# Prompt attention and sample attention of a decoder step in one written-out pipeline of 80 units

## The chip, the core and the metric

The kernel runs on one NeuronCore of a Trainium2 chip. The metric is device time in microseconds (us), median of three runs. The engines, each with a queue of its own: TensorE (PE, with its weight loads as PEld), VectorE (DVE), ScalarE (ACT), GpSimd (POOL) and SyncE (SP, which only starts transfers here). They meet at semaphores. Matmul results go to eight banks of PSUM, 512 fp32 values per partition each.

## The reference, cut to what matters

The model is a two-layer decoder step for a prompt of 1040 tokens (16 learned ones and 1024) and, with the same weights, eight samples of 8 new tokens over 512 cached ones. Layer 0 has a convolution branch and an attention branch of 8 heads of width 64:

```
s = einsum('bqhd,bkhd->bhqk', q, k) * 64**-0.5      # and a bias c_q - c_k per head, c = cumsum(log forget gate)
p = softmax(where(pos_k <= pos_q, s + bias, -inf))
att = einsum('bhqk,bkhd->bqhd', p, v)               # prompt: 1040 x 1040 causal; sample: 8 x 520, cache read through a page table
conv_out = silu(layer_norm(depthwise(a)))           # over 512 channels
mix = concat([conv_out, att]) @ w_out               # then residual, layer norm, SwiGLU, layer norm
```

Layer 1 has other mixers and is not touched. Outputs are fp32.

## The kernel before, in words

Activations lie transposed, channels on partitions, T = 1104 columns (1040 of the prompt, 64 of the samples), in three chunks of C = 368. Large products split each fp32 operand into a high and a low fp32r part and run three matmuls (`mm3`, L670 to L672). The program is in stages: input and projections; keys and values written out; prompt attention; sample attention; output product; SwiGLU; layer 1.

**Prompt attention.** A unit is one head and one tile of 128 queries (tile 8 has 16): `att_units`, 72 units, with the keys up to the diagonal, 128 to 1040 of them. Every engine runs the same step number n over all units, written out, and in order:
- PE: `scores` of unit n (L823, L825 for the mask, L827; fp32r) into banks 0-2 or 3-5 in turn; `turn` of unit n-2 (L840: transposes of the exponentials through banks 5 and 6); `values` of unit n-3 (L859: transposed probabilities as 128-column weights, 64 value columns moving, into bank 2 or 7 in turn); and at some steps `back` (L868), a transpose of a finished 128-column result of two heads.
- DVE: `inverse` (L1681) of the row sum of unit n-1, `peak` (L1677, the row maximum) of unit n, `turned` (L1687, a PSUM copy), parts of the next head's operands (`head_low`, L1497, L1707, L1710) and the copy behind `back` (L1695).
- ACT: `expo` (L1186) of unit n, `turned` (L1193) for bank 6, `result` (L1200), which scales the value product by the inverse row sum, and `head_high` (L1211).
- POOL does nothing in it (255.7 us without work).

**Sample attention** comes after it and takes one sequence at a time, in loops: 32 transposes of cached keys (`turn_keys`, L895) copied by ACT (L1241); `sample_scores` (L907 to L909); maximum (DVE L1742), exponential (ACT L1245), normalisation (DVE L1747); transposes (L918), copies (ACT L1250); `sample_values` (L925: the cache's values as 128-column weights, 16 columns moving). Between them stands the layer norm of the convolution branch, chunk by chunk (products L684 and L685 with a matrix of 1/512, DVE L1755, L1758, L1762, ACT L1274, L1277, and Silu L1281). Its buffers lie where those of prompt attention were, so SP starts the cache's loads when that has ended.

**Output product** (`out_product`): four pairs of input tiles in the order OUT_TILES[0] = (0, 1, 2, 3), where 0 and 1 are the convolution's and 2 and 3 the attention's. ACT rounds them to the high part (L1292), DVE makes the low part (L1497). The first weights are split long before.

Of the kernel before, what the change touches and what calls it, by code (L numbers as in the profile page):

```python
# [14 lines left out]
P = 128  # L15
# [48 lines left out]
OUT_TILES = ((0, 1, 2, 3), (0, 2, 1, 3))  # L64
# [7 lines left out]
PV0 = 64 * (NPAGE + 1)  # L72
ORDER = (tuple(range(9)), (0, 8, 1, 2, 3, 4, 5, 6, 7))
# [26 lines left out]
def build(nc, t):  # L100

    ctx = ExitStack()
    with ctx:
# [27 lines left out]
        SSM, _ = at("SSM", o, [P, HT, NS, NQ])  # L131
# [5 lines left out]
        SELC, _ = at("SELC", o, [P, NS, NH, NQ])  # L137
# [10 lines left out]
        YSM, o = at("YSM", o, [P, 2, C])  # L148
# [3 lines left out]
        ATT, o = at("ATT", B0 + 8 * T * 4, [P, 2, NTT, P])  # L152
        assert o <= R0
        YCA, o = at("YCA", B0 + 8 * T * 4, [P, HT, C])
        SQA, o = at("SQA", o, [P, HT, C])
        YSA, o = at("YSA", o, [P, 2, C])
        RSA, o = at("RSA", o, [P, C])
# [16 lines left out]
        QS1, o = at("QS1", A0, [P, 2, TP], F32R)  # L174
        KS1, o = at("KS1", o, [P, 2, TP], F32R)
        QS2, o = at("QS2", o, [96, 2, TP], F32R)
        PB, o = at("PB", o, [P, 3, TP])
        assert o >= stage_end
        VP, o = at("VP", o, [P, 2, NTT, P])
        PT, o = at("PT", o, [P, 2, NTT, P])  # L180
        KS2, o = at("KS2", o, [96, 2, TP], F32R)
        QBA, o = at("QBA", o, [32, TP])
        IDR, o = at("IDR", o, [P, P], F32R)
        MKR, o = at("MKR", o, [P, P], F32R)
        ST4, o = at("ST4", o, [P, 3, 72])
        LFO, o = at("LFO", o, [P, NTT, NH])
        assert o <= B0

        KR, o = at("KR", A0, [P, 2, NPAGE, HALF])
        VR, o = at("VR", o, [P, 2, NPAGE + 1, HALF])  # L190
        KTS, o = at("KTS", o, [P, 2, HT, KS])
        PSA, o = at("PSA", o, [64, 2, KS])
        PTS, o = at("PTS", o, [P, 2, NPAGE + 1, 64])
        QBD, o = at("QBD", o, [P, 2, 328])
        LFS, o = at("LFS", o, [64, KS])
        KBS, o = at("KBS", o, [P, KS])
        SLS, o = at("SLS", o, [P, 2, 64])
        CQ2, o = at("CQ2", o, [P, NQ])
        ST5, o = at("ST5", o, [64, 2, 8])
        assert o <= B0  # L200
# [46 lines left out]
        def row(k, r):  # L247
# [23 lines left out]
        qk_done, nm_ready, exp_done, rc_ready = sem("qk_done"), sem("nm_ready"), sem("exp_done"), sem("rc_ready")  # L271
        back_done, back_evac = sem("back_done"), sem("back_evac")
# [4 lines left out]
        kr_in, vr_in = [sem("kr_in0"), sem("kr_in1")], [sem("vr_in0"), sem("vr_in1")]  # L277
        sk_done, kt_ready, kt_new, qbd_zero, qbd_ready, sls_ready = (sem("sk_done"), sem("kt_ready"), sem("kt_new"),
                                                                     sem("qbd_zero"), sem("qbd_ready"), sem("sls_ready"))
        sqk_done, snm, sexp, s_inverse, spn = sem("sqk_done"), sem("snm"), sem("sexp"), sem("s_inverse"), sem("spn")  # L280
        spt_done, spt_ready, spv_done, satt = sem("spt_done"), sem("spt_ready"), sem("spv_done"), sem("satt")
        la_sum, la_mean, la_cen, la_sq, la_sum2, la_var, la_sd, la_rs, la_nrm, la_act, la_hi = (
            sem("la_sum"), sem("la_mean"), sem("la_cen"), sem("la_sq"), sem("la_sum2"), sem("la_var"), sem("la_sd"),
# [39 lines left out]
        def att_units():  # L323

            na = nb = 0
            for u in range(72):
                h, i = u // 9, ORDER[(u // 9) % 2][u % 9]
                groups = (i + 4) // 4
                yield u, h, i, (P if i < 8 else META), min(P * (i + 1), TP), na, nb
                na += 1 + (groups > 2)  # L330
                nb += groups > 1
# [6 lines left out]
        def backs_until(n):  # L338

            return sum(b <= n for b in BACKS)  # L340

# [1772 lines left out]
```

## Time and profile before

| | us |
|---|---|
| median of 3 runs (2873.38 to 2879.08) | 2873.52 |
| the profiled execution, device time | 2870.65 |
| its span in the profile | 2869.0 |
| PE busy | 2697.3 (94%) |
| DVE busy | 1348.7 (47%) |
| ACT busy | 747.0 (26%) |
| POOL busy | 341.0 (12%) |
| first score matmul to first matmul of the output product | 323.81 to 740.40 |

### The profile page before, as it was taken

What the parts mean: (1) busy time and instruction counts of PE and PEld (TensorE: products, weight loads), DVE (VectorE), ACT (ScalarE), POOL (GpSimd) and SP (SyncE); (2) the same over time, 40 slices, a digit from 0 to 9 for tenths busy, and PEclk for the clock granted to TensorE, in tenths of its full rate; (3) what the DMA queues carried; (4) which work ended last, traced back from release to release, by engine and by line L of the source; (5) the groups of instructions that cost most, each with busy time, mean ns of one, the idle gap of its engine ahead of it and who ended that gap; (6) DMA issues with size and microseconds to landing.
All of it is one profiled execution on the core that took longest, in us unless ns stands there. A gap on an engine that the chain in (4) does not pass through costs nothing.

```text
span 2869.0 us, 39072 instructions
## 1 busy us (share of the span) xinstructions
PE 2697.3 (94%) x15849; PEld 2593.0 (90%) x15849; DVE 1348.7 (47%) x2024; ACT 747.0 (26%) x1273; POOL 341.0 (12%) x329
## 2 busy tenths in 40 slices
PE   8999698888989999999999999998999999999996
PEld 7998577655879999999999999998999999999996
DVE  4788666311576333333333565377633333323356
ACT  3111466333234111111111252233411111111124
POOL 3298000000120000000000220022000000000022
PEclk9999799877899999999999999999999999999998
DMA  7110200234102111111111131130111111111101
GB/s 221 48 44 15 82 8 9 78 95 142 34 15 60 45 45 45 43 39 45 38 45 45 45 101 45 44 111 20 54 45 45 38 45 38 45 45 45 45 15 63
DMA packets 165323, 152.52 MB, mean 53 GB/s; under 512 B 8609, under 2 KB 140049, under 8 KB 165144
## 3 DMA queue, kind: packets, MB, share of 16 engines
q1 hardware_dynamic: 157632, 133.92, 15.5%
q0 software_dynamic: 6208, 15.94, 1.7%
q8 instruction: 132, 2.16, 0.3%
q10 hardware_dynamic: 1320, 0.24, 0.1%
q14 instruction: 31, 0.25, 0.0%
HBM read 131.43 MB, written 18.93 MB: 52 GB/s over the span
## 4 chain that ended last, share of the span: by engine, by line
PE 86%; DVE 7%; issue 3%; ACT 2%; DMA 1%; SPq 0%; ACTq 0%; DVEq 0%; POOL 0%; POOLq 0%
PE PS L670 26%; PE PS L671 25%; PE PS L672 25%; PE PS L925 2%; PE PS L859 2%; DVE ST L1677 1%; PE PS L907 1%; PE PS L840 1%; PE PS L684 1%; PE PS L678 1%; PE PS L685 1%; DVE RSD L1786 1%; DVE SPR L1603 0%; DVE PT L1687 0%; PE PS L823 0%
## 5 line engine op out<-in xcount | busy, mean ns | idle before, releaser
L670 PE MATMUL PS<-AH,WHI 128*128 128x368 f32 x3360 | 1124.2, 335 | 30.4 <-issue 15.4
L672 PE MATMUL PS<-AH,WLO 128*128 128x368 f32 x3360 | 1113.3, 331 | 4.5 <-issue 4.5
L671 PE MATMUL PS<-AL,WHI 128*128 128x368 f32 x3360 | 1116.8, 332 | 0.0
L670 PEld LDWEIGHTS PS<-AH,WHI 128*128 128x128 f32 x3360 | 637.0, 190 | 45.1 <-issue 23.2
L671 PEld LDWEIGHTS PS<-AL,WHI 128*128 128x128 f32 x3360 | 635.9, 189 | 3.0 <-issue 0.8
L672 PEld LDWEIGHTS PS<-AH,WLO 128*128 128x128 f32 x3360 | 636.3, 189 | 0.0
L1878 DVE TENSOR_TENSOR HF<-S,PS 128x368 f32<-128x368 f32 x132 | 70.9, 537 | 707.2 <-ACT S L1118 707.2
L670 PE MATMUL PS<-HH,WHI 128*128 128x368 f32 x1056 | 349.8, 331 | 3.4 <-DVE Y L1889 3.4
L671 PE MATMUL PS<-HL,WHI 128*128 128x368 f32 x1056 | 349.6, 331 | 0.0
L672 PE MATMUL PS<-HH,WLO 128*128 128x368 f32 x1056 | 349.3, 331 | 0.0
L1889 DVE TENSOR_TENSOR Y<-Y,PS 128x368 f32<-128x368 f32 x480 | 251.5, 536 | 154.9 <-PE PS L672 154.9
L1118 ACT ACTIVATE S<-PS 128x368 f32<-128x368 f32 x156 | 74.7, 479 | 907.1 <-PE PS L672 907.0
L597 POOL TENSOR_TENSOR YSM<-Y 128x736 f32<-128x736 f32 x12 | 21.3, 1776 | 1629.2 <-DVE Y L1889 1438.0
L1497 DVE TENSOR_TENSOR WLO<-RAW,WHI 128x1024 fp32r<-128x1024 f32 x164 | 199.1, 1244 | 21.7 <-ACT WHI L1396 18.1
L1396 ACT CAST WHI<-RAW 128x1024 fp32r<-128x1024 f32 x108 | 107.9, 1047 | 374.6 <-PE PS L672 374.6
L670 PEld LDWEIGHTS PS<-HH,WHI 128*128 128x128 f32 x1056 | 198.6, 188 | 5.2 <-DVE Y L1889 4.9
L672 PEld LDWEIGHTS PS<-HH,WLO 128*128 128x128 f32 x1056 | 198.6, 188 | 0.0
L671 PEld LDWEIGHTS PS<-HL,WHI 128*128 128x128 f32 x1056 | 198.2, 188 | 0.2
L1591 DVE SCALAR_TENSOR_TENSOR PS<-AEXT,PRT,PS 128x1040 f32<-128x1040 f32 x87 | 113.4, 1304 | 2.3
L1497 DVE TENSOR_TENSOR HL<-HF,HH 128x368 fp32r<-128x368 f32 x132 | 77.1, 584 | 74.8 <-ACT HH L1375 74.8
L1849 DVE TENSOR_TENSOR Y<-Y,PS 128x368 f32<-128x368 f32 x144 | 75.3, 534 | 55.5 <-PE PS L672 55.2
L859 PE MATMUL PS<-VP,PT 128*128 128x64 f32 (+2 forms) x720 | 93.1, 283 | 3.6 <-DVE QKV L1695 3.4
(260 smaller groups left out, 2366.3 us busy)
## 6 DMA issues: line engine op xcount, KB each, us to landing
RAW<-in_w_ffn_gate SPq DMA_DIRECT2D x44, 512.0 KB, 4.0
RAW<-in_w_ffn_up SPq DMA_DIRECT2D x44, 512.0 KB, 4.9
RAW<-in_w_ffn_down SPq DMA_DIRECT2D x44, 512.0 KB, 3.5
RAW<-in_w_in_even SPq DMA_DIRECT2D x20, 512.0 KB, 4.8
Y<-x_spill SPq DMA_DIRECT2D x16, 552.0 KB, 5.6
KR<-in_cache_k SPq DMA_DIRECT2D x32, 256.0 KB, 3.3
VR<-in_cache_v SPq DMA_DIRECT2D x32, 256.0 KB
RAW<-in_w_in_odd SPq DMA_DIRECT2D x16, 512.0 KB, 4.7
```

Of the source, the lines that this page charges most:

```text
L670: pe.matmul(out, wh, xh, start=first, stop=False)
L671: pe.matmul(out, wh, xl, start=False, stop=False)
L672: return pe.matmul(out, wl, xh, start=False, stop=last)
L859: mm = pe.matmul(PS[0:m, (2, 7)[u % 2], 0:HD], PT[0:kw, u % 2, jt, 0:m], VP[0:kw, h // 2 % 2, jt, HD * (h % 2):HD * (h % 2 + 1)], start=(j ...
L925: mm = pe.matmul(PS[:, 6, PV0 + 16 * c:PV0 + 16 * c + 16], VR[0:kw, j, g, c * P:(c + 1) * P], PTS[0:kw, j, g, 16 * c:16 * c + 16], start=( ...
L1118: act.activation(s_tile[:, par, :] if bank0_to is None else bank0_to, PS[:, 2 * par, 0:C], func).then_inc(s_ready, 1)
L1396: act.copy(WHI[:, 2 * s1 % 4 + e, :], RAW[:, 2 * s1 % 4 + e, :]).then_inc(w_hi, 1)
L1497: return dve.tensor_tensor(out, x, f32(hi), ALU.subtract)
L1591: dve.scalar_tensor_tensor(acc, src, row(k, R_DW + j), acc, ALU.mult, ALU.add).then_inc(acc_step, 1)
L1849: dve.tensor_tensor(y, y, PS[:, 4 + n % 3, 0:C], ALU.add).then_inc(d_free, 1)
L1878: dve.tensor_tensor(HF[:, par, :], S[:, par, :], PS[:, 2 * par + 1, 0:C], ALU.mult).then_inc(gu_free, 1)
L1889: dve.tensor_tensor(y, y, PS[:, 4 + n % 3, 0:C], ALU.add).then_inc(d_free, 1)
```

## The change

Prompt and sample attention become one pipeline of 80 units, ten per head: tiles 0 to 5, then the sample sequence with the head's number (`None` in ORDER), then tiles 6, 8 and 7. What differs:

- A unit is normalised before its transposes: POOL multiplies the exponentials in place by the inverse row sum (new, all 80 units), and `turn` waits for it (`pn_ready`).
- The value product is turned round: values are the weights (64 columns), transposed probabilities move (128 columns), the result comes out transposed. `back`, its copies and the tile ATT are gone; ACT copies the result (64 x 128) straight to QKV. Its PSUM is bank 7 alone.
- On PE the value product of unit n-3 stands before the transposes of unit n-2, no longer behind.
- The cached keys of sequence s are turned in steps 10s+2 to 10s+5, one `turn_keys` a step, through bank 6. Its softmax goes through `peak`, `expo` and `inverse` as the prompt's. Cache buffers are single now, and lie over the weight buffers WHI and WLO.
- The statistics of the convolution's layer norm are spread over the steps from 10 on; one Sqrt for all chunks, the inverses (DVE), the scaling (now POOL) and Silu come after the last unit, beside the output product, whose order is now (2, 3, 0, 1).
- As WHI and WLO are taken, the first output weights are split after the last unit, no longer in the projection stage.

```
-OUT_TILES = ((0, 1, 2, 3), (0, 2, 1, 3))
+OUT_TILES = ((2, 3, 0, 1), (0, 2, 1, 3))
-ORDER = (tuple(range(9)), (0, 8, 1, 2, 3, 4, 5, 6, 7))
+ORDER = (0, 1, 2, 3, 4, 5, None, 6, 8, 7)
+NU = NH * len(ORDER)
...
+            for u, h, i, m, n, _, _ in UNITS:
+                gp.wait_ge(rc_ready, u + 1)
+                gp.nop(nofuse=True)
+                gp.tensor_scalar(PB[0:m, u % 3, 0:n], PB[0:m, u % 3, 0:n], ST4[0:m, 2, u:u + 1], 1.0, ALU.mult, ALU.mult).then_inc(pn_ready, 1)
+                if u % 10 == 3:
+                    new_keys(h)
...
             def turn(u, h, i, m, n, na, nb):
-                pe.wait_ge(exp_done, u + 3)
+                pe.wait_ge(pn_ready, u + 1)
...
             def values(u, h, i, m, n, na, nb):
+                pe.wait_ge(att_evac, u + 1)
...
-                if u > 1:
-                    pe.wait_ge(att_evac, u)
...
-                    mm = pe.matmul(PS[0:m, (2, 7)[u % 2], 0:HD], PT[0:kw, u % 2, jt, 0:m],
-                                   VP[0:kw, h // 2 % 2, jt, HD * (h % 2):HD * (h % 2 + 1)], start=(jt == 0), stop=(jt == i))
+                    mm = pe.matmul(PS[0:HD, 7, 0:m], VP[0:kw, h // 2 % 2, jt, HD * (h % 2):HD * (h % 2 + 1)], PT[0:kw, u % 2, m * jt:m * jt + m],
+                                   start=(jt == 0), stop=(jt == i))
...
+            for n in range(NU + 3):
+                if n < NU:
+                    if UNITS[n][2] is None:
+                        sample_scores(n, UNITS[n][1], *UNITS[n][5:])
+                    else:
+                        scores(*UNITS[n])
                 if n >= 3:
                     values(*UNITS[n - 3])
+                if 2 <= n < NU + 2:
+                    turn(*UNITS[n - 2])
+                if key_turn(n):
+                    turn_keys(*key_turn(n))
...
+            for n in range(NU + 3):
+                if n < NU:
                     expo(*UNITS[n])
...
+                if 2 <= n < NU + 2:
                     turned(*UNITS[n - 2])
+                if key_turn(n):
+                    keys(*key_turn(n))
+                if n < NU and n % 10 == 2:
+                    queries(n // 10)
...
                 if n >= 3:
                     result(*UNITS[n - 3])
...
+                if n < NU - 10 and n % 10 in (5, 6, 7, 8):
+                    head_high(n // 10 + 1, n % 10 - 5)
```

The first part is POOL's, then come PE's `turn`, `values` and its loop, and last ACT's loop.

Three places in the program. PE in a steady part of prompt attention before, tiles 6 and 7 of a head (VP and PT are values and transposed probabilities, CST holds the identity):

```order
L823 MATMUL PS<-KS,QS 128x512
L827 MATMUL PS<-KS,QS 128x512
L823 MATMUL PS<-KS,QS 128x512
L825 MATMUL PS<-MKR,IDR 128x128
L827 MATMUL PS<-KS,QS 128x512
L840 MATMUL PS<-CST,PB 128x128 x6
L859 MATMUL PS<-VP,PT 128x64 x5
L868 MATMUL PS<-CST,ATT 128x128
```

PE in the changed kernel at the same tile 7, with the sample's value product (VR holds the cached values):

```order
L842 MATMUL PS<-KS,QS 128x512
L846 MATMUL PS<-KS,QS 128x512
L842 MATMUL PS<-KS,QS 128x512
L844 MATMUL PS<-MKR,IDR 128x128
L846 MATMUL PS<-KS,QS 128x512
L900 MATMUL PS<-PT,VR 128x16 x20
L888 MATMUL PS<-CST,PB 128x128 x7
L842 MATMUL PS<-KS,QS 128x128
```

The value product moved in front of the transposes, `back` is gone, and the sequence's value product stands among the prompt's units.

PE before, in the stage of the samples, from one value product to the next sequence's scores (YSA holds the convolution's sums, QBD the queries):

```order
L925 MATMUL PS<-PTS,VR 128x16 x20
L684 MATMUL PS<-YSA,CST 128x368
L685 MATMUL PS<-YSA,CST 128x368
L899 REGISTER_ALU
L901 ISA
L907 MATMUL PS<-KTS,QBD 64x512 x4
L908 MATMUL PS<-KBS,SLS 64x512
L907 MATMUL PS<-KTS,QBD 64x8 x4
```

PE in the changed kernel, the step in front of the sequence's scores and these:

```order
L911 MATMUL PS<-PT,VP 64x128 x3
L888 MATMUL PS<-CST,PB 128x128 x4
L868 MATMUL PS<-CST,KR 128x128 x4
L859 MATMUL PS<-KTS,QBD 64x512 x4
L860 MATMUL PS<-KBS,SLS 64x512
L859 MATMUL PS<-KTS,QBD 64x8 x4
L860 MATMUL PS<-KBS,SLS 64x8
```

The last quarter of the cached keys is turned directly before the scores that need its copy.

ACT in the changed kernel, steps 6 to 8 of a head (PB are the exponentials):

```order
L1180 ACTIVATE PB,ST_111<-PS,ST_111 64x520
L1187 COPY PT<-PS 128x128
L1212 ACTIVATE QKV<-PS 64x128
L1222 ACTIVATE QS_94<-QKV 64x1040
L1180 ACTIVATE PB,ST_111<-PS,ST_111 128x896
L1187 COPY PT<-PS 128x256
L1212 ACTIVATE QKV<-PS 64x128
L1222 ACTIVATE KS_98<-QKV 64x1040
L1180 ACTIVATE PB,ST_111<-PS,ST_111 16x1040
```

The result copy (L1212), for which PE's next value product waits, stands behind the exponential of a unit three places newer.

## Rows read from the trace of the kernel before

**Rows 1.** The page: granted clock of PE in 40 slices, in tenths.

```profile
PEclk9999799877899999999999999999999999999998
```

**Rows 2.** Stretches: length, busy of each engine, clock, DMA share, GB/s.

```profile
323.80:540.40 216.60, 194.19 (x1412) 170.87 (x1412) 128.72 (x271) 122.59 (x284) 0.00 (x0) 0.90 0.02 6
...
550.00:740.40 190.40, 156.09 (x689) 111.17 (x689) 31.47 (x43) 61.22 (x131) 13.41 (x22) 0.72 0.34 114
```

**Rows 3.** PE in order of time: start, us, line; idle before in brackets.

```profile
323.81 0.44 PE L823 MATMUL PS<-KS,QS 128*128 128x128 f32 x1 [9.37 <-DVE QS L1710]
...
447.95 0.39 PE L823 MATMUL PS<-KS,QS 128*16 128x512 f32 x1 [1.59 <-ACT ATT L1200]
...
479.16 1.23 PE L859 MATMUL PS<-VP,PT 128*128 128x64 f32 x10
...
502.49 0.39 PE L823 MATMUL PS<-KS,QS 128*16 128x512 f32 x1 [1.58 <-ACT ATT L1200]
...
740.40 0.64 PE L670 MATMUL PS<-AH,WHI 128*128 128x368 f32 x1 [2.39 <-issue]
```

**Rows 4.** Waits, 320 to 541 us: us in total, times, longest.

```profile
PE PS L840 <- DVE PT L1687: 9.4, 18, 0.9
...
PE PS L823 <- ACT ATT L1200: 8.3, 8, 1.7
```

**Rows 5.** Waits, 541 to 740 us.

```profile
PE PS L918 <- DVE PSA L1747: 24.5, 8, 5.6
...
PE PS L895 <- DMA KR<-in_cache_k: 5.4, 1, 5.4
...
DVE KBS L1733 <- DMA LFS<-lf_spill: 4.3, 1, 4.3
```

**Rows 6.** One sequence in order of time, all engines.

```profile
556.12 3.65 PE L907 MATMUL PS<-KTS,QBD 128*64 128x512 f32 x8 [0.68 <-ACT KTS L1241]
...
561.29 1.97 PE L895 MATMUL PS<-CST,KR 128*128 128x128 f32 x16
...
564.72 0.48 PE L918 MATMUL PS<-CST,PSA 64*128 64x64 f32 x5 [1.46 <-DVE PSA L1747]
...
565.84 7.26 PE L925 MATMUL PS<-PTS,VR 128*128 128x16 f32 x40 [0.64 <-ACT PTS L1251]
...
573.03 1.59 PE L684 MATMUL PS<-YSA,CST 128*128 128x368 f32 x2
```

**Rows 7.** Clock around a value product of the samples, 2 us each.

```profile
566.00:568.00 2.00, 2.00 (x18) 1.95 (x18) 0.00 (x0) 0.00 (x0) 0.00 (x0) 1.00 0.00 0
...
570.00:572.00 2.00, 2.00 (x10) 1.93 (x10) 0.00 (x0) 0.00 (x0) 0.00 (x0) 0.50 0.00 0
...
576.00:578.00 2.00, 2.00 (x3) 0.53 (x3) 1.75 (x2) 1.03 (x2) 0.00 (x0) 0.50 0.80 249
...
580.00:582.00 2.00, 2.00 (x12) 0.83 (x10) 0.00 (x0) 0.00 (x0) 0.50 (x1) 1.00 0.96 338
```

**Rows 8.** Groups by form, 320 to 541 us.

```profile
L1186 ACT ACTIVATE PB<-PS,ST 128x1024 f32<-128x1024 f32 x8 | 8.9, 1114 | 9.0 <-DVE ST L1677 9.0
L1677 DVE TENSOR_REDUCE ST<-PS 128x1 f32<-128x896 f32 x8 | 8.6, 1072 | 0.0
```

**Rows 9.** POOL in order of time, beside the projections.

```profile
204.85 0.70 POOL L539 TENSOR_SCALAR S<-AEXT,PRT 128x520 f32<-128x520 f32 x1
...
207.05 2.61 POOL L539 TENSOR_SCALAR S<-AEXT,PRT 128x520 f32<-128x520 f32 x1
```

**Rows 10.** DVE in the same stretch.

```profile
206.49 2.68 DVE L1497 TENSOR_TENSOR WLO<-RAW,WHI 128x1024 fp32r<-128x1024 f32 x2
```

**Rows 11.** Groups by form, 541 to 740 us.

```profile
L1758 DVE RECIPROCAL RSA<-RSA 128x368 f32<-128x368 f32 x3 | 7.4, 2453 | 37.4 <-ACT RSA L1277 37.4
```

**Rows 12.** Groups by form, 740 to 830 us.

```profile
L1103 ACT ACTIVATE WHI<-RAW,WMN 128x1024 fp32r<-128x1024 f32 x6 | 6.9, 1154 | 0.2
L1099 ACT ACTIVATE WHI<-RAW 128x1024 fp32r<-128x1024 f32 x6 | 6.3, 1051 | 36.0 <-PE PS L672 36.0
```

More of the change, by code:

```diff
@@ L583, in _ @@
+            for q in range(2):
+                for c in range(NC):
+                    gp.wait_ge(la_rs, c + 1)
+                    rows = AEXT[:, 2 * q:2 * q + 2, chunk(c)]
+                    gp.tensor_tensor(rows, rows, RSV[:, c, :].unsqueeze(1).to_broadcast([P, 2, C]), ALU.mult).then_inc(la_nrm, 1)
             parts = [0]
@@ L861, in values, with conv_norm @@
                 mm.then_inc(pv_done, 1)
[L863 to L874 removed]
+            def conv_norm(c, s_in, s_res, wide):
+                if wide >= 0:
+                    pe.wait_ge(exp_done, wide + 3)
+                norm_product(ONES_H, YSA, s_in, s_res, c, 2)
@@ L875, in _ @@
                 if n >= 3:
                     values(*UNITS[n - 3])
-                if n in BACKS:
-                    back(*BACKS[n], units=n - 3)
-            for k, x in enumerate(LATE):
-                back(*x, bank=(7, 2)[k % 2], left=1 if k else 0, units=72)
-            pe.wait_ge(back_evac, HT * NTT)
-            pe.wait_ge(lfr_in, 16 * NS * NPAGE)
-            u = TU_LFS
-            transposes(u, 6, [(PS[0:64, 6, g * P:(g + 1) * P], LFR[:, g, :, :].rearrange("p s h -> p (s h)"), IDN) for g in range(NPAGE)])
@@ L1091, in _, with split_centred @@
             centred = [0]
[L1093 to L1095 removed]
+            def split_centred(stage, js=(0, 1)):
+                for n in [2 * stage + j for j in js]:
                     pos, i = n % 4, centred[0] + 1
@@ L1290, in _, with mix_high @@
+            def mix_high(q, src):
                 for c in range(NC):
-                    src = AEXT if q < 2 else QKV
                     act.copy(AH[:, 2 * q:2 * q + 2, chunk(c)], src[:, 2 * q % 4:2 * q % 4 + 2, chunk(c)]).then_inc(la_hi, 1)
+            act.wait_ge(qk_done, NU)
+            act.wait_ge(att_evac, 1 + NU)
+            mix_high(2, QKV)
+            mix_high(3, QKV)
+            split_centred(ST_OUT0 + 1)
+            for k in range(HT):
+                act.wait_ge(la_nrm, 3 * (k // 2 + 1))
+                act.activation(AEXT[:, k, 0:T], AEXT[:, k, 0:T], ACT.Silu, bias=row(k, R_LAB), scale=row(k, R_LAG)).then_inc(la_act, 1)
@@ L1294, in squares @@
+            for q in range(2):
+                act.wait_ge(la_act, 2 * q + 2)
+                mix_high(q, AEXT)
             def squares(ln, c, qs=range(4)):
@@ new lines, in inverse_conv @@
+            def inverse_conv(c):
+                dve.wait_ge(la_sd, 1)
+                dve.reciprocal(RSV[:, c, :], RSV[:, c, :]).then_inc(la_rs, 1)
+            for n in range(NU + 3):
+                if 1 <= n < NU + 1:
+                    inverse(*UNITS[n - 1])
+                if n < NU:
+                    peak(*UNITS[n])
+                if 2 <= n < NU + 2:
+                    turned(*UNITS[n - 2])
+                if n == 1:
+                    select()
+                c = norm_step(n, 13)
+                if c is None:
+                    c = norm_step(n, 14)
+                if c is not None:
+                    q = n % 10 - 3
+                    qs = slice(2 * q, 2 * q + 2)
+                    dve.wait_ge(la_mean, c + 1)
+                    dve.tensor_tensor(AEXT[:, qs, chunk(c)], AEXT[:, qs, chunk(c)], two(PS[:, 2, 0:C]), ALU.subtract).then_inc(la_cen, 1)
+                if n < NU - 10 and n % 10 in (6, 7, 9):
+                    head_low(n // 10 + 1, (6, 7, 9).index(n % 10))
+                if n > NU:
+                    inverse_conv(n - NU - 1)
```

532 lines of the change are left out of this document (232 added, 300 removed).

## The prediction

> **What bounds the kernel now.** I read the granted clock first, then the busy time of each engine by stretch, then the start times of single matmuls, and the waits last. The slices show a clock of 7 or 8 tenths between 280 and 720 us and 9 nearly everywhere else [rows 1]. The stretches say what stands there: prompt attention (216.6 us, PE busy 194.2, clock 0.90) and the stage of the samples (190.4 us from 550 on, PE busy 156.1, clock 0.72), with DVE at 128.7 and 31.5 us and ACT at 122.6 and 61.2 [rows 2]. No engine but PE is near its limit, and PE is slowed by its clock and by waits. The whole stretch that the change rewrites goes from the first score matmul at 323.81 to the first matmul of the output product at 740.40, 416.6 us; inside prompt attention the same tile of a head comes back after two heads at 447.95 and 502.49, so a head takes 54.54 / 2 = 27.3 us [rows 3]. Eight of these are 218, the rest, some 199 us, is sample attention, the convolution's norm and the changeover.
>
> In prompt attention PE waits for copies out of PSUM: 9.4 us for DVE's copy behind the transposes and 8.3 us for ACT's result, 17.7 in all or 2.2 a head [rows 4]. In the stage of the samples it waits 24.5 us in eight pieces of 5.6 at most for the normalised exponentials, because only one sequence is in flight, and 5.4 once for the first cached keys, whose load begins when prompt attention has ended [rows 5].
>
> **The change, term by term.** I keep the 27.3 us of a head and add what PE gets on top, at full clock.
> - Keys of a sequence: 16 transposes in 1.97 us less the pipeline's tail, 0.11 each: +1.8 [rows 6].
> - Scores of a sequence: from 556.12 to the transposes at 561.29: +5.2 [rows 6].
> - Transposes of its probabilities: +0.5 [rows 6].
> - Its value product, 40 records: 18 start in 2.00 us at clock 1.00, so 0.11 each: +4.4. At clock 0.50 it is 10 in 2.00 [rows 7].
> - The norm's products: six pairs. Two records take 1.59 us at clock 0.50 [rows 6, 7], a pair is four records, some 2.8, half of that at full clock: 6 x 1.4 / 8 = +1.0.
> - `back`, 4.5 transposes a head at 0.11: -0.5.
> - The prompt's value product: a record had a load of 128 columns and 64 moving, now 64 and 128. The transposes have 128 moving columns and start every 0.11 [rows 6]; ten value records of the prompt take 1.23 us with the tail of the last, the same distance [rows 3]. So I count 0; the bounds are 72 records a head times 0.02 either way, 1.4 a head.
>
> Sum: 27.3 + 1.8 + 5.2 + 0.5 + 4.4 + 1.0 - 0.5 = 39.7 us a head.
>
> The Trainium skill ("TensorE: Matmul & The Clock Gate", LDWEIGHTS (loading the stationary operand)) says that a load costs by its columns, not its rows. By that alone a value record with 64 weight columns would halve, 3.9 us a head or 31 in all; the transposes, which move 128 columns and do not start closer than 0.11, say that the moving side holds it at the old price, and the sum goes by them.
>
> Waits. The 2.2 us a head go: the transposes now have a value product in front of them while the copy runs, and the wide unit no longer needs a bank of a result. New ones come. The value product has one bank, so it needs the result copy of the unit before, which ACT issues behind an exponential three units newer. Behind this on PE's queue are the transposes, for which DVE and ACT wait, and so the next value product. Price: peak up to 1.07, exponential up to 1.11 with its sum, a PSUM copy and the result under 1 together [rows 8], some 3 us from the end of the scores; PE has in that time the value product, the transposes, a quarter of the keys and the next scores. For tiles 6, 8, 7 that is 3 us or more. For tiles 2 to 4 it is 1.5 to 2.5, so I put 0.7 on three steps. The scores of a sequence stand directly behind the last quarter of its keys, whose copy comes behind the exponential of tile 5: 1.2 more. 3.3 - 2.2 = +1.1. Bounds: -2.2 (all covered) and +10 (1 us and more in each of ten steps).
>
> Clock. In the samples' value product the clock fell to 0.50 some 3.5 us after its start and was back at 1.00 only after 578, in the next scores, though PE's busy column stays 2.00 of 2.00 [rows 7]. In prompt attention 0.90 on average cost 0.10 x 216.6 / 8 = 2.7 a head [rows 2], and stays in the 27.3. The value product of a sequence still stands in one piece in every head, and the narrow tile 8 comes directly behind it, so half-speed stretches of some 8 us a head are to be expected, 4 us lost. +1.6 over the 2.7, with the bounds -2.7 (never falls) and +8 (half of a head at 0.50).
>
> A head is then 39.7 + 1.1 + 1.6 = 42.4, eight are 339.
>
> POOL's new operation: 0.70 us for 128 x 520; it grows to about 1.3 for 1040 if it goes by the elements. One took 2.61, while DVE ran two subtractions with both inputs in SBUF [rows 9, 10]; DVE has two of these per head here. Ten units come to 8 to 12 us of 42, and the chain from the scores to the transposes (peak, exponential, inverse, POOL; up to 4.5) lies inside two steps of PE (4 to 9). I count 0. Uncovered it would be 1 us in the short steps, 3 to 4 a head, and at the 2.61 in each unit 26 a head, still no bound. ACT gets 122.6 + 61.2 less some 16 for Silu, roots and tables, DVE less than 160 [rows 2]: half of 339.
>
> The start. DVE now makes the samples' running sums ahead of the first peak, and waited 4.3 for the load behind them [rows 5]; this load starts earlier than the first scores, so about 3 us of it show, with the first keys' load of 5.4 beside it: +3 (bounds 1 and 7). The end. The first output weights are rounded by ACT only now: two times 1.15 + 1.05 [rows 12] and two small ones, 5.2 us, between the last copies; DVE has two inverses of 2.45 [rows 11] and two low parts in front of its first low part of the attention. PE has some 6 us of transposes and value products to cover 13: +7 (bounds 4 and 15). It replaces the 2.39 that is in the 740.40 [rows 3]. What remains of the convolution (11 us on POOL, Silu, rounding, about 30 in a row) has the first half of the output product in front of it, 48 units of nearly 1 us: 0.
>
> New stretch: 3 + 339 + 7 = 349 against 416.6, a gain of 67 us. Profiled execution: 2870.65 - 67 = 2803; its device time lies 2.9 under the median shown, so the forecast is **2806 us**.
>
> **Rivals.**
> - *A: the clock holds and waits are covered.* For it: PE has more dense work than before, and the turned value product moves twice the columns. Against: the samples' value product is unchanged, and the clock fell in each that I looked at. Head 39.7 - 2.2 - 1 = 36.5: stretch 302, time 2759. The Trainium skill (same page, Part 1: The HAM clock gate) says that what releases and lowers the clock is how busy PE is; by the busy column it could not fall in that product. By that rule this case is right; rows 7 speak against it. 20%.
> - *B: ACT and PE step together.* The one bank of the result makes PE wait some 0.8 us in nearly every step, 6 to 7 a head instead of 3.3, and the tile after it starts late too. For it: the 8.3 us of PE's waits for that copy before, with two banks [rows 4]. Head 47: stretch 386, time 2843. 17%.
> - *C: slower.* The result's bank closes a ring: scores, peak, exponential, result, next value product, in series. For a wide unit nearly 1 for the scores, 1.1 and 1.3 for peak and exponential [rows 8], 0.4, 1.0 and four hand-overs of 0.1 are 5.2 us. If each of 80 steps costs this, the stretch is 426 and the time 2883. It decides from a mean step of (416.6 - 10) / 80 = 5.1 us, where mine is 4.2. Against: the scores of the next unit and the transposes run between the links, and short tiles have links of 0.3 to 0.5. 4%.
> - *D: nothing gained*, since the cached keys, or the loads of x_spill that now run beside the last head, come late: one buffer of keys instead of two, but seven steps (over 20 us) for a load of some 6. 2%.
>
> **How the numbers follow.** Forecast 57%, A 20, B 17, C 4, D 2. The forecast's own range is 2780 to 2828. The range to 8 in 10 takes most of A and of B: 2755 to 2846. This kernel's runs tell some 0.2%, 6 us, from no change. Faster: forecast, A and B, 94%; same 2%; slower 4%.
>
> **What would show it.** Right: from the first score matmul to the first of the output product 335 to 365 us; steps of ten units 40 to 45 us apart; the clock at 0.50 once a head, beginning in the samples' value product; no wait of PE for POOL above 1 us in a step; PE's waits mostly for ACT's result copy and, once a head, for the last copy of the keys; a gap of about 7 us ahead of the output product. A clock near 1.00 through a head says A. A wait for the result in nearly all steps says B, and one as long as peak and exponential together C. Wrong at its base would be a head that is bound by ACT, DVE or POOL.

## The result, and the profile after

The changed kernel takes 2834.3 us (median, 2830.2 to 2838.6), the one before 2876.3 beside it: ratio 0.9853, 95% interval 0.9832 to 0.9874, 42 us or 1.5% faster. 2806 was forecast. Between the two profiled executions 36.2 us of span went (2869.0 to 2832.8), where 67 were forecast.

The slices of the page, each a fortieth of the span, busy tenths of PE and its granted clock:

```profile
PE   8999699998889999999999999998999999999996
...
PEclk9999778797999999999999999999999999999998
```

Five slices at 7 and 8 stand in that region, as many as before [rows 1]. The stretch from the first score matmul to the first matmul of the output product, whole, and below it four pieces of one head (columns: length, busy us and count of PE, its weight loads, DVE, ACT and POOL, granted clock, DMA share, GB/s):

```profile
324.34:710.05 385.71, 349.24 (x2081) 278.81 (x2081) 155.18 (x291) 169.29 (x391) 79.46 (x104) 0.82 0.19 62
452.00:454.00 2.00, 2.00 (x17) 1.92 (x17) 0.00 (x0) 0.21 (x2) 0.00 (x0) 1.00 0.00 0
454.00:456.00 2.00, 2.00 (x10) 1.92 (x10) 0.00 (x0) 0.00 (x0) 0.00 (x0) 0.50 0.00 0
468.00:470.00 2.00, 2.00 (x9) 1.67 (x9) 0.69 (x3) 0.99 (x3) 0.48 (x1) 0.50 0.00 0
472.00:474.00 2.00, 2.00 (x11) 1.47 (x12) 0.36 (x2) 1.21 (x4) 0.59 (x1) 1.00 0.00 0
```

The stretch takes 385.7 us where it took 416.6 and where 349 were forecast. The clock is at half from 454 to 471, 17 us of one head. In each of the eight heads it falls while the samples' value product runs, and in two of them once more. The starts on PE that measure a head (start, duration, line, tiles, shape, pause before it and what ended it): the first scores of the samples in two heads, and the output product.

```profile
386.98 1.07 PE L859 MATMUL PS<-KTS,QBD 128*64 128x512 f32 x2 [0.68 <-ACT KTS L1192]
...
434.86 1.07 PE L859 MATMUL PS<-KTS,QBD 128*64 128x512 f32 x2 [0.68 <-ACT KTS L1192]
...
710.05 0.65 PE L685 MATMUL PS<-AH,WHI 128*128 128x368 f32 x1 [4.60 <-DVE WLO L1495]
```

These two are 47.9 us apart, where 42.4 were forecast for a head; the eight lie 45.2 to 47.9 apart. What PE waited for between 326 and 711 (tile of the waiting matmul, releaser, us in total, times, longest), the answer to [rows 4, 5]:

```profile
PE PS L911 <- ACT QKV L1212: 13.3, 21, 0.9
PE PS L842 <- issue: 6.8, 7, 1.0
PE PS L859 <- ACT KTS L1192: 5.4, 8, 0.7
PE PS L685 <- DVE WLO L1495: 4.6, 1, 4.6
PE PS L900 <- ACT QKV L1212: 2.0, 3, 0.7
PE PS L842 <- ACT PB L1180: 1.7, 1, 1.7
PE PS L868 <- DMA KR<-in_cache_k: 1.3, 1, 1.3
PE PS L911 <- ACT QKV L1209: 0.9, 1, 0.9
```

They are 36.0 us in all, where the same sum was 60.3 before. L911 is the prompt's value product, L900 that of the samples, L888 the prompt's transposes, L842 to L846 the scores, L685 the output product.

So the stretch is read with three numbers: its length, PE's waits in it, and the half-speed time, which is 2 x (1 - granted clock) summed over windows of 1 us; half of that is lost. Before: 416.6 us, 60.3 waited, 157 at half speed, so 78.5 lost and a rest of 277.8 (work at full clock). After: 385.7, 36.0, 140 and so 70.0 lost, rest 279.7.

Half of it is an upper figure, because a pause of PE is not made longer by a slow clock, and this count takes a pause inside a half-speed stretch twice. Two of the changed kernel's half-speed stretches, whole (length, then PE's busy time):

```profile
454.01:471.08 17.07, 16.09 (x82) 14.53 (x82) 4.11 (x11) 3.49 (x13) 3.68 (x4) 0.50 0.22 64
686.12:710.05 23.93, 17.09 (x88) 15.25 (x87) 11.12 (x11) 13.88 (x24) 5.24 (x3) 0.50 0.08 23
```

PE is busy for 123.3 of the 140 us here, and for 141.9 of 157 before. Half of the busy part, 61.6 and 70.9 us, is lost, and the rest becomes 288.1 and 285.4. So some 9 us of the gain come from the clock and 24 from the waits, less some 3 of added work. In the table below the count with the whole half-speed time is kept for all kernels; the lost time read from it is too high by 1 to 8 us. What follows the stretch is 5.9 us shorter (2128.6 to 2122.8), PE's busy time there 5.2 shorter, and in its first 460 us the clock is 0.99 instead of 0.98. I did not follow this part further.

### The profile page after: what moved, and what is told of

Read it like the earlier page. It is cut to its first block, busy times and chain, and to the rows that moved or that the text cites. A ratio compares the mean times of both kernels' runs of the same rounds, so it can differ in the third digit from the quotient of the medians.

```text
span 2832.8 us, 38745 instructions
## 1 busy us (share of the span) xinstructions
PE 2688.7 (95%) x15813; PEld 2582.7 (91%) x15813; DVE 1347.8 (48%) x1990; ACT 730.8 (26%) x1242; POOL 413.2 (15%) x415
## 4 chain that ended last, share of the span: by engine, by line
PE 88%; DVE 6%; ACT 2%; issue 2%; DMA 1%; SPq 0%; DVEq 0%; POOL 0%; ACTq 0%
PE PS L685 26%; PE PS L686 25%; PE PS L687 25%; PE PS L911 3%; PE PS L900 2%; PE PS L888 2%; PE PS L859 1%; PE PS L693 1%; DVE AL L1484 1%; DVE ST L1662 1%; DVE SPR L1590 1%; ACT PB L1180 1%; PE PS L842 1%; DVE RSD L1767 1%; PE PS L846 0%
## 5 line engine op out<-in xcount | busy, mean ns | idle before, releaser
L685 PE MATMUL PS<-AH,WHI 128*128 128x368 f32 x3360 | 1122.2, 334 | 36.6 <-DVE Y L1830 15.7
L685 PEld LDWEIGHTS PS<-AH,WHI 128*128 128x128 f32 x3360 | 634.7, 189 | 47.7 <-DVE Y L1830 19.7
L1860 DVE TENSOR_TENSOR HF<-S,PS 128x368 f32<-128x368 f32 x132 | 70.9, 537 | 694.4 <-ACT S L1114 694.4
L685 PE MATMUL PS<-HH,WHI 128*128 128x368 f32 x1056 | 349.8, 331 | 3.3 <-DVE Y L1871 3.2
L1871 DVE TENSOR_TENSOR Y<-Y,PS 128x368 f32<-128x368 f32 x480 | 251.5, 536 | 154.9 <-PE PS L687 154.9
L1484 DVE TENSOR_TENSOR WLO<-RAW,WHI 128x1024 fp32r<-128x1024 f32 x164 | 199.1, 1243 | 21.7 <-ACT WHI L1383 18.1
L685 PEld LDWEIGHTS PS<-HH,WHI 128*128 128x128 f32 x1056 | 198.6, 188 | 5.0 <-DVE Y L1871 4.8
L911 PE MATMUL PS<-PT,VP 128*64 128x128 f32 (+2 forms) x720 | 110.5, 308 | 14.5 <-ACT QKV L1212 13.3
L911 PEld LDWEIGHTS PS<-PT,VP 128*64 128x64 f32 (+1 forms) x720 | 92.4, 170 | 27.5 <-ACT QKV L1212 20.3
```

The source lines that it names most:

```text
L685: pe.matmul(out, wh, xh, start=first, stop=False)
L911: mm = pe.matmul(PS[0:HD, 7, 0:m], VP[0:kw, h // 2 % 2, jt, HD * (h % 2):HD * (h % 2 + 1)], PT[0:kw, u % 2, m * jt:m * jt + m], start=(jt ...
L1484: return dve.tensor_tensor(out, x, f32(hi), ALU.subtract)
L1860: dve.tensor_tensor(HF[:, par, :], S[:, par, :], PS[:, 2 * par + 1, 0:C], ALU.mult).then_inc(gu_free, 1)
L1871: dve.tensor_tensor(y, y, PS[:, 4 + n % 3, 0:C], ALU.add).then_inc(d_free, 1)
```

## The experiments

All against the changed kernel unless said. The table has the ratio to the kernel before with its interval, then from the profiled run the stretch, PE's waits and the half-speed time.

| kernel | median us | ratio [95%] | stretch | waits | at half speed |
|---|---|---|---|---|---|
| before | 2876.3 | 1 | 416.6 | 60.3 | 157 |
| changed | 2834.3 | 0.9853 [0.9832, 0.9874] | 385.7 | 36.0 | 140 |
| e1_cols64 | 2826.3 | 0.983 [0.9802, 0.9857] | 377.3 | 35.7 | 108 |
| e2_quarter | 2784.3 | 0.9688 [0.9662, 0.9714] | 328.2 | 39.2 | 62 |
| e3_turn_first | 2787.0 | 0.9692 [0.9667, 0.9717] | 337.0 | 16.2 | 67 |
| e4_two_halves | 2832.3 | 0.9851 [0.9825, 0.9877] | 383.5 | 29.1 | 148 |
| e5_first_samples | 2810.5 | 0.9753 [0.9731, 0.9775] | 367.4 | 25.5 | 118 |
| e6_first_others | 2809.2 | 0.975 [0.9729, 0.977] | 362.2 | 23.0 | 110 |
| e7_first_cols64 | 2787.4 | 0.968 [0.966, 0.970] | 338.3 | 16.4 | 65 |
| e8_first_cols64_end | 2789.1 | 0.9672 [0.9642, 0.9702] | 340.3 | 14.4 | 72 |
| e9_first_dense | 2824.9 | 0.9833 [0.9803, 0.9863] | 371.9 | 16.9 | 106 |
| e10_first_tiles | 2824.6 | 0.9831 [0.9802, 0.9861] | 379.3 | 18.1 | 161 |
| e11_dense | 2866.7 | 0.9983 [0.997, 0.9996] | 407.1 | 35.7 | 144 |
| e12_first_pauses | 2817.2 | 0.9785 [0.9761, 0.9808] | 364.9 | 30.4 | 99 |

My first theory was that the samples' value product sets off the half-speed stretch because its records move 16 columns each; the rivals were the result's one bank, and the weight loads.

**e1_cols64.** The records of the samples' product move 64 columns.

```diff
-mm = pe.matmul(PS[:, 7, 16 * c:16 * c + 16], VR[0:kw, g, c * P:(c + 1) * P],
-               PT[0:kw, u % 2, 64 * g + 16 * c:64 * g + 16 * c + 16], ...)
+mm = pe.matmul(PS[:, 7, 64 * c:64 * c + 64], VR[0:kw, g, c * P:(c + 1) * P],
+               PT[0:kw, u % 2, 64 * g:64 * g + 64], ...)
```

> The samples' value product moves 64 columns of probabilities per record instead of 16 (same 40 records and weights; the 48 others are computed and not read). Theory 1 (the clock falls because these records stream so few columns, and a head then runs 17 of 47.8 us at 0.50): the records stay at 0.11 us, the half-speed stretch goes or shrinks, 35 to 65 us faster than the changed kernel's 2834, i.e. 2770 to 2800. Rival 2 (the shortfall is waits for the result's one bank, or the turned product's price): no change, 2834 +- 5, clock as before. Rival 3 (the clock falls because of the many weight loads, whatever moves): no change either, the trace shows 0.50 in the same places.

8 us faster at the median, with a ratio whose interval overlaps that of the changed kernel. The half-speed time fell from 140 to 108, the stretch by 8.4, and the mean granted clock of the whole program was 0.966 or 0.967 in all four runs, where the changed kernel's four had 0.962 to 0.965. This lies between the theories: in this order more columns a record did give back some clock, but not most of it.

**e2_quarter.**

```diff
-                    for c in range(HT):
+                    for c in range(1):
```

> Leaves out three of the four column groups of the samples' value product, 30 of its 40 records in each head. Theory 1: besides 30 x 0.11 = 3.3 us a head of work at full clock, the half-speed stretch behind it (8.5 us lost a head) goes: 8 to 12 us a head, 2740 to 2770. Rival 2: only the records' own time goes, 3.3 to 5 us a head, 2795 to 2808, and the clock still falls in the narrow tile or the transposes behind it.

This leaves out three quarters of the product, so its time only measures what the product costs. 2784, 50 us faster, between the two forecasts: the stretch lost 57.5. Half-speed time given back is 78 / 2 = 39 of it, the 240 records at 0.13 are 31, less 3 more of waiting. These sum to 67, 10 too many, and about half of that are the pauses at half speed that the count takes twice. 8 to 12 a head were expected of theory 1, 7.2 came. But the fall is not gone. With ten records instead of forty, in the head at 395 (same columns as above):

```profile
397.00:399.00 2.00, 1.24 (x8) 0.83 (x7) 1.26 (x2) 1.61 (x5) 0.00 (x0) 0.65 0.36 100
401.00:403.00 2.00, 2.00 (x11) 1.94 (x10) 0.00 (x0) 0.00 (x0) 0.00 (x0) 0.50 0.28 107
405.00:407.00 2.00, 2.00 (x17) 1.78 (x17) 0.42 (x1) 0.56 (x2) 0.19 (x1) 0.50 0.00 0
409.00:411.00 2.00, 1.98 (x9) 1.58 (x8) 0.86 (x3) 0.92 (x3) 0.48 (x1) 0.50 0.00 0
```

The product is over at 397.0, the clock falls within the next microsecond and stays at 0.50 for 14 us, through transposes and prompt value products. In this head and one more it is 14 us, in five others 3 to 7, in one none. A long product makes the fall longer or likelier, and a short one does not keep it away.

**e3_turn_first.** This undoes one part: on PE the transposes stand in front of the value product again.

```diff
+                if 2 <= n < NU + 2:
+                    turn(*UNITS[n - 2])
                 if n >= 3:
                     values(*UNITS[n - 3])
-                if 2 <= n < NU + 2:
-                    turn(*UNITS[n - 2])
```

> PE's value product stands behind the transposes again instead of in front of them, everything else as in the changed kernel. The forecast's step (2.2 us a head of waits for the copies behind the transposes go with the new order): 10 to 20 us slower than the changed kernel, 2845 to 2854, the value products waiting for DVE's copy. Rival: the older unit's copy was made long ago either way (the product is one unit late now), so no change, 2834 +- 5, or a little faster, since the result's copy gets more time.

The main expectation had the wrong sign, and by far, and its rival (no change or a little faster) was too small: 2787, 47 us faster than the changed kernel and 3.1% faster than before. The stretch:

```profile
325.43:662.42 336.99, 320.50 (x2080) 254.58 (x2081) 152.72 (x291) 169.01 (x392) 79.12 (x104) 0.90 0.22 71
440.00:442.00 2.00, 2.00 (x16) 1.92 (x15) 0.00 (x0) 0.27 (x2) 0.00 (x0) 0.98 0.00 0
442.00:444.00 2.00, 2.00 (x15) 1.85 (x15) 0.75 (x4) 0.78 (x4) 0.26 (x1) 0.50 0.64 162
448.00:450.00 2.00, 2.00 (x23) 1.77 (x21) 0.76 (x2) 1.07 (x3) 0.48 (x1) 0.81 0.00 0
```

and its waits from 326 to 663:

```profile
PE PS L859 <- ACT KTS L1192: 5.6, 8, 0.7
PE PS L685 <- DVE WLO L1495: 5.5, 1, 5.5
PE PS L911 <- ACT QKV L1212: 3.1, 8, 0.5
PE PS L842 <- ACT PB L1180: 1.8, 1, 1.8
PE PS L868 <- DMA KR<-in_cache_k: 0.2, 1, 0.2
```

Two things went. The waits: 36.0 to 16.2. No wait for DVE's copy behind the transposes came back, so the place of the value product in front is not what took it away. Nor is it the product's age, as the expectation has it: PE takes the product of unit n-3 in all three kernels. The run does not show what did it. And the clock: 140 us at half speed became 67. It now falls when the samples' product ends and stays down for 6.5 to 7 us in seven heads of eight, where it was 10 to 17 in seven and 24 in the last. Counted by PE's busy time, 32 us are lost and the rest is 289, so 20 us of waits and 30 of clock, less 1 of other work, are the 48.7 us that the stretch lost. Why the place in front makes waits is in DVE's queue. First the changed kernel, then this one (start, duration, instruction, pause before it):

```profile
449.75 1.23 DVE L1662 TENSOR_REDUCE ST<-PS 128x1 f32<-128x1024 f32 x1 [0.24 <-PE PS L846]
456.53 0.69 DVE L1675 COPY PT<-PS 128x512 f32<-128x512 f32 x1 [5.56 <-PE PS L888]
457.26 0.75 DVE L1694 TENSOR_SCALAR QS<-QBA,CST 32x1040 fp32r<-32x1040 f32 x1
```

```profile
435.89 1.23 DVE L1662 TENSOR_REDUCE ST<-PS 128x1 f32<-128x1024 f32 x1 [0.43 <-PE PS L846]
437.03 0.68 DVE L1675 COPY PT<-PS 128x512 f32<-128x512 f32 x1
437.74 0.75 DVE L1694 TENSOR_SCALAR QS<-QBA,CST 32x1040 fp32r<-32x1040 f32 x1
```

In the changed kernel DVE idles 5.56 us, because the transposes stand behind the samples' product; then it copies them and only after that makes the last operand of the next head's scores. PE waits 0.98 us for this at each head's first scores, the 6.8 us of "issue". With the transposes first that operand is ready at 438.5, 3 us ahead of the next scores. The 13.3 us at L911 are the other half: a value product directly behind the scores asks for the result's bank earlier by the time of the transposes (0.76 us for seven), and ACT's copy is not there yet.

**e4_two_halves.** Even units write partitions 0 to 63 of the result's bank, odd ones 64 to 127. The samples' unit needs the whole bank, so it and the unit behind it still wait for the last copy.

```diff
-                pe.wait_ge(att_evac, u + 1)
+                pe.wait_ge(att_evac, u + (u % 10 in (6, 7)))
-                    mm = pe.matmul(PS[0:HD, 7, 0:m], ...)
+                    mm = pe.matmul(PS[HD * (u % 2):HD * (u % 2 + 1), 7, 0:m], ...)
```

> The prompt's value products write partitions 0 to 63 of the result's bank for even units and 64 to 127 for odd ones, so a product waits for the copy of the unit before last, not the last. PE waits 2.0 us a head for that copy in the changed kernel's trace. Theory 1: at most these 2.0 go, 8 to 16 us in all, 2818 to 2826. Rival B of the prediction (the one bank makes ACT and PE step together): 4 us a head or more, below 2805. Third case: the wait only moves to the transposes or scores, 2834 +- 4.

2832, no change, as in the third case: the 13.3 us at L911 went, but 4.8 of them came back as waits for ACT's copy of the transposes, so 6.9 less in all, and 8 us more at half speed took 4 of it back. The one bank is worth 3 us here, and rival B falls. Fewer pauses did not shorten the half-speed time.

**e5_first_samples and e6_first_others.** The 47 us of the order are parted: transposes first only in the step with the samples' product, and only in the nine others.

```diff
+                turn_first = n % 10 == 9        # e6: n % 10 != 9
```

> Only in the one step of ten that holds the samples' value product do the transposes stand in front of it; in the nine others the value product stays in front. The kernel with the transposes first everywhere took 2787, the changed one 2834; its trace has 70 us at half speed against 140 and some 17 us less waiting. Theory 1 (the 47 us are mostly the clock, and this one step sets it off): 25 to 40 us of them come back, 2795 to 2810, half-speed time 70 to 90 us. Rival (they are waits for the result's copy in the nine other steps): 2825 to 2834, half-speed time stays near 140.

> The reverse: transposes first in nine steps of ten, the samples' value product still in front of the transposes in its step. Theory 1: only the waits for the result's copy go (12.9 us in the changed kernel's trace, 2.8 with the transposes first): 2818 to 2828, half-speed time still 110 us or more. Rival: 2787 to 2800.

24 and 25 us: each gives half. e5 stands at the edge of its theory 1 in time (2810.5) and outside it in half-speed time (118 and not 70 to 90), e6 between its two forecasts. e5 takes away 10.5 us of waits (the 6.8 and the 2.0 at L900 are gone) and 22 us at half speed, 11 lost; e6 13.0 us of waits and 30 at half speed, 15 lost. In both the lost clock goes down with the waits, though the product's forty records are the same.

**e7_first_cols64 and e8_first_cols64_end.** Transposes first with 64 columns a record, and in e8 DVE makes the first output weights' low parts before the norm's inverses.

```diff
                 if n > NU:
-                    inverse_conv(n - NU - 1)
-            split_centred(ST_OUT0)
+                    split_centred(ST_OUT0, (n - NU - 1,))
...
-                if o == 2:
-                    inverse_conv(NC - 1)
+                if o in (2, 3, 4):
+                    inverse_conv(o - 2)
```

> Transposes first in all steps and the samples' value product with 64 moving columns a record. With 16 columns and transposes first 2787 with 70 us at half speed; 64 columns alone took the changed kernel's half-speed time from 140 to 107 us and gave 8 us. If both shorten the same stretches: 2780 to 2786. If the number of streamed columns decides: the fall of 7 us a head goes wholly, 2755 to 2775. If the order alone decides: 2787 +- 3.

> As the kernel with transposes first and 64 columns, and DVE makes the low parts of the first output weights before the norm's three inverses, not behind two of them. The gap of PE ahead of the output product, 4.6 to 5.5 us for that low part, loses the 4.75 us of two inverses as far as ACT's rounding allows (it ends 1.1 us before DVE starts now, so some 2.5 to 3.5 us): 2 to 4 us below the kernel without it. If the norm's inverses then come late for the second half of the output product, no gain.

e7 is e3 again: 2787.4, 65 us at half speed against 67. With the transposes first, four times the columns change nothing. In e8 the gap ahead of the output product went from 5.5 to 2.3 us as expected:

```profile
665.42 0.41 PE L685 MATMUL PS<-AH,WHI 128*128 128x368 f32 x1 [2.26 <-issue]
```

but its total is no lower, with single runs from 2778 to 2792. The half-speed time was 7 us longer in this run, so 3 us can't be told here.

**e9_first_dense and e11_dense.** Eight dense matmuls a head stand inside the samples' product, in the order of e3 and in that of the change.

```diff
+                            if g in (1, 3):
+                                pe.wait_ge(exp_done, u + 5)
+                                mm = pe.matmul(PS[:, 2, :], QS1[:, h % 2, 0:P], KS1[:, h % 2, 0:512], start=True, stop=True)
```

> Transposes first in all steps, and eight added matmuls of 512 moving columns a head, two after each ten records... of the samples' value product (their result is never read). Their own cost is 8 x 0.24 = 1.9 us a head, 15 us in all. In the kernel without them the clock is at 0.50 for 7 us right behind each product (67 us in all). If sparse streaming in the product sets the fall off: it goes, 33 us come back, net 10 to 18 us faster than 2787. If the fall has another cause: 2800 to 2806, half-speed time as before.

> The changed kernel (value product in front of the transposes) with the eight added matmuls of 512 columns a head inside the samples' value product. They cost 15 us. Theory 1 (sparse product sets off the 17 us at half speed a head, 140 us in all): half-speed time falls below 50 us, 45 us come back, 2798 to 2812, and the order's 47 us shrink to the waits, some 15. Theory 2 (the order itself, by the waits it makes, brings the clock down): half-speed time stays above 110 us, 2840 to 2850.

Both are slower than anything forecast: e9 by 38 us on e3, e11 by 32 on the changed kernel, where their own work was put at 15. Of the 35 us that e9's stretch grew, 15 are that work and 19 are lost to more time at half speed. e11's half-speed time stayed at 144, as its theory 2 has it; its profiled run is the fastest of ten (2861), so its row in the table is not quite its median's. In e9 the clock still falls:

```profile
446.00:448.00 2.00, 2.00 (x14) 1.59 (x13) 0.99 (x3) 1.08 (x3) 0.78 (x1) 1.00 0.00 0
448.00:450.00 2.00, 2.00 (x13) 1.56 (x12) 0.00 (x0) 0.00 (x0) 0.34 (x1) 0.98 0.00 0
450.00:452.00 2.00, 2.00 (x8) 1.85 (x8) 0.00 (x0) 0.00 (x0) 0.00 (x0) 0.50 0.00 0
458.00:460.00 2.00, 2.00 (x10) 1.67 (x9) 0.00 (x0) 0.27 (x1) 0.44 (x1) 0.50 0.23 88
```

It falls some 5 us after the product's start, as in e3, and stays down 10 us instead of 7 (10 to 14 in the eight heads). My first theory is dead in this form: more streamed columns in the product do not hold the clock. The page of the Trainium skill that the prediction named for rival A ("TensorE: Matmul & The Clock Gate", Part 1: The HAM clock gate) has busy-ness set the clock; these rows, with PE busy 2.00 of 2.00 on both sides of the fall, show that the busy column at least does not tell when it falls.

**e10_first_tiles.**

```diff
-ORDER = (0, 1, 2, 3, 4, 5, None, 6, 8, 7)
+ORDER = (6, 1, 2, 3, 4, 5, None, 0, 8, 7)
```

> Transposes first in all steps, and in the order of the tiles 0 and 6 change places, so that the scores of tile 6 (896 columns) and not of tile 0 (128) stand behind the samples' value product, and tile 0's product in place of tile 6's. If the half-speed stretch lasts as long as the sparse work behind the product: 7 us a head become 3.5 or none, 10 to 25 us faster than 2787. If it lasts by itself: 2787 +- 5. If the wide tile at the head's start waits for the next head's operands or peak: 2790 to 2800.

38 us slower than e3, outside all three forecasts, and 161 us at half speed, the most of all, with hardly more waiting (18.1 against 16.2). The half-speed stretch is 17 to 20.5 us long in seven heads of eight, and runs on into the end of the attention in the last. A wide tile's scores behind the samples' product do not bring the clock back. So the order of the tiles alone can cost as much clock as the order of the product and the transposes gave. Which of the two exchanged tiles does it was not tried.

**e12_first_pauses.** From e9 to e11 a third theory was left: pauses. The kernel before has them in front of falls in prompt attention (the pauses of 1.59 and 1.58 us at 447.95 and 502.49 too [rows 3]). Its PE there:

```profile
392.00:394.00 2.00, 0.52 (x3) 0.28 (x4) 0.57 (x3) 1.33 (x4) 0.00 (x0) 1.00 0.00 0
394.00:396.00 2.00, 2.00 (x14) 1.73 (x13) 1.32 (x2) 0.06 (x1) 0.00 (x0) 0.65 0.00 0
396.00:398.00 2.00, 2.00 (x11) 2.00 (x11) 0.66 (x2) 1.51 (x3) 0.00 (x0) 0.50 0.00 0
```

PE did 0.52 us of work in two, and a microsecond later the clock fell, with no sample product near. So two pauses went into e3:

```diff
+                    pe.wait_ge(pta_ready, UNITS[u + 1][5] + 2)   # ahead of the samples' product
...
+                    if n and n % 10 == 0:
+                        pe.wait_ge(att_evac, n - 2)              # ahead of a head's first scores
```

> Transposes first in all steps, and two waits added per head that PE does not need: ahead of the samples' value product it waits for DVE's copy of the transposes just made (about 1 us), and ahead of the next head's first scores for ACT's copy of that product (about 0.9 us). They stand where the changed kernel's PE has its waits of 0.7 and 0.98 us. By themselves they cost 8 x 1 + 7 x 0.9 = 15 us on 2787: 2802. Theory 3 (formed from the runs so far: it is the pauses on PE around this product, not its sparse records, that lengthen the half-speed stretch behind it): 25 to 35 us more, 2825 to 2840, and the half-speed stretches grow from 7 us a head to 10 to 17. Rival (the place of the product in the order matters by itself): 2800 to 2805, stretches of 7 us as before.

2817, 30 us slower than e3, between the two forecasts. The waits are 30.4, 14.2 more, and the half-speed time 99, 31 more, 16 lost: 30 together, where the stretch grew by 28. The stretches at half speed are 10 to 10.5 us in seven heads, where e3 had 6.5 to 7:

```profile
443.00:445.00 2.00, 0.91 (x8) 0.67 (x6) 1.82 (x2) 1.37 (x2) 1.03 (x1) 1.00 0.00 0
447.00:449.00 2.00, 2.00 (x14) 1.95 (x13) 0.00 (x0) 0.00 (x0) 0.26 (x1) 0.74 0.00 0
449.00:451.00 2.00, 2.00 (x10) 1.93 (x10) 0.00 (x0) 0.00 (x0) 0.00 (x0) 0.50 0.00 0
455.00:457.00 2.00, 2.00 (x11) 2.00 (x10) 0.05 (x1) 0.00 (x0) 1.78 (x2) 0.50 0.84 289
```

The two pauses together cost themselves and about as much again in clock. That did not reach the 25 to 35 us of clock that I expected on top, nor the changed kernel's 140 us at half speed. So pauses at this place are a part of the cause. They are not all of it: e10 has more half-speed time with hardly more pauses, and e4 with fewer.

The best kernels that leave nothing out are e3, e7 and e8, at 0.967 to 0.969 of the time before, which no interval tells apart; e3 is the simplest. It is the change without its reordering of value product and transposes. Its other parts (POOL's normalisation, the turned value product, the samples' units) were not undone one by one.

## Why the prediction was right and wrong

- *Direction and range* held: 2834 lies in 2755 to 2846, and a faster kernel had 94%. The range held by luck, though: 2834 is outside the forecast's own 2780 to 2828 and inside the wide one only because that takes in rival B, which did not occur. Two of the signs of "right" failed as well, the stretch (385.7, not 335 to 365) and the heads (45 to 48, not 40 to 45). The source of the gain held: the 24.5 us that PE waited for one sequence's probabilities and the 9.4 for DVE's copies [rows 4, 5] are gone.
- *Work.* 39.7 a head less the 2.2 of waits and 2.7 of clock inside it is 34.8, 278 for eight. The rest of the stretch measured 279.7, but 288.1 with the pauses at half speed counted once, so the work was put some 10 us too low. The turned value product was put at nothing. Ten of its records are followed by the next matmul 1.07 us after their start before the change (479.16 [rows 3] to the first line), 1.24 after it:

```profile
480.23 0.28 PE L868 MATMUL PS<-CST,ATT 128*128 128x128 f32 x1
...
442.69 1.31 PE L911 MATMUL PS<-PT,VP 128*64 128x128 f32 x10
443.93 0.87 PE L888 MATMUL PS<-CST,PB 128*128 128x128 f32 x6
```

Within a product the records start 0.109 us apart instead of 0.106, and the rest is lost once per product. Over the nine tiles of a head, at full clock, it is 10.3 us against 8.9, some 1.3 more, inside the stated bound of 1.4. The samples' product is 0.13 a record at full clock, not 0.11, 5.2 us a head instead of 4.4:

```profile
436.45 5.23 PE L900 MATMUL PS<-PT,VR 128*128 128x16 f32 x40
```

- *Waits.* 3.3 a head new; measured in the heads 13.3 + 6.8 + 5.4 + 2.0 + 0.9 = 28.4, or 3.5. (The recorded 1.07 us for the longest peak is tile 6's; tile 7's takes 1.21.) Start 3.0 (1.7 + 1.3) against +3, end 4.6 against +7. Right in size, in part by luck: the wait of each head's first scores for DVE's last operand was not in my list, and the start's 1.7 are a wait for the first exponentials, while the load behind the running sums kept DVE for 0.3 us only. And the reason given for the old 2.2 going, that "the transposes now have a value product in front of them", was wrong for DVE's copies: e3 has the transposes in front again, no such wait either, and 19.8 us fewer of all.
- *POOL* at nothing was right: PE's weight loads waited 0.3 us for it in all. Its operation took 1.12 us for the widest tiles against the estimated 1.3:

```profile
L580 POOL TENSOR_SCALAR PB<-PB,ST 128x1024 f32<-128x1024 f32 x8 | 9.0, 1122 | 64.6 <-DVE ST L1666 64.6
...
L580 POOL TENSOR_SCALAR PB<-PB,ST 128x128 f32<-128x128 f32 x8 | 3.0, 374 | 34.2 <-DVE ST L1666 34.2
```

- *Clock: the step that failed.* "half-speed stretches of some 8 us a head are to be expected, 4 us lost. +1.6 over the 2.7" makes 34 us lost in the stretch. 70 were lost by the same count, 62 with the pauses taken out: 28 to 36 of the 37 us between 349 and 385.7. The 8 us came from one sequence of the old stage [rows 7], where pauses and short steps stood elsewhere, and the order had no part in them. The whole stage [rows 2] had a better price: at a clock of 0.72 over 190.4 us 53 us were lost there, 6.7 a sequence; with the 2.7 that makes 9.4 a head, 75 in all. The upper bound of +8 a head held it. e3 has 67 us at half speed, 34 lost: the term would have been right for that order.
- *Rival B* named nearly the stretch measured (386) by the wrong road. It wanted 6 to 7 us of waits a head; there were 3.5, and e4 shows that a freer bank gives 2 us in the total, which is within the noise. A number that fits is no proof of its mechanism.
- *Rival A*: the clock did not hold in any kernel here. C and D did not occur.

**What stays open.** Which work or pause sets the fall, and which brings the clock back. The streamed columns of the product do not with the transposes first (e7, e9), and in the changed order 64 columns a record took a part of it away (e1) where dense matmuls did not (e11). The product's length matters (e2) but does not settle it. Waits do in part (e12, e5, e6), not in e4, and the order of the tiles does by some other road (e10). The Trainium skill ("TensorE: Matmul & The Clock Gate", Part 4: PE-mode transpose) says that transposes do not count as busy in the way that other matmuls do; no run here took the transposes away to try that. In a kernel the clock also tends to fall at the same place in head after head (406, 454, 502 and 550 us in the changed one); whether a small shift of the work alone would change a stretch's length was not tried.

## What to carry to other kernels

When a stretch has phases at half clock, put a price on them for the new order, not the one of the old: here it was 60 to 70 us, about twice the estimate, and some 30 of the 48 us that the order on PE decided in the stretch. In front of a long product that nobody waits for, put the short work that other engines wait for; behind it, their queues idle and hand the pause back to PE. The two pauses added around this product cost about their own length again in clock (e12); that is no rule, since e4 took pauses away and won nothing in clock. Before keeping a change of several parts, undo each part alone: one reordering cost 47 us here, and all the rest together gained 88.

## What the hardware showed that I had not expected

- The granted clock falls to 0.50 with PE busy 2.00 of 2.00 us and stays there through 13 us of matmuls without a pause (in the stretch from 454 to 471 above, after one pause of 0.98 us that ends at 458.1). Stretches at half speed lasted from 3 to 27 us in these kernels.
- Eight more dense matmuls a head made the half-speed time longer, not shorter: 106 us against 67.
- Turning the value product round (64 weight columns and 128 moving for 128 and 64) left the distance of its records as it was, 0.109 against 0.106 us, and cost some 0.15 us once per product.
- A value record of the samples with 64 moving columns costs hardly more than one with 16: forty take 5.55 us (e7) against 5.23 (e3).
- Two halves of a result bank, one per 64 partitions, can be filled and emptied in turn by PE and ACT, and a single bank is then enough for two results.
